# Gated linear attention: where a chunk's state work stands on VectorE, and ACT's copy of the turned keys

## The chip, the core and the metric

One core of one Trainium2 chip runs one program. The metric is the device time of the whole program in microseconds (us), the median of several executions. Names of engines: TensorE is PE, VectorE is DVE, ScalarE is ACT, GpSimd is POOL, SyncE is SP.

## The reference, cut to what matters

The program computes two layers of a trunk; layer 1 has, beside a recurrent branch (LRU), a gated linear attention (GLA) in both directions, over 1024 latent tokens and 128 context tokens. The change touches only the GLA chunks of that layer. What they compute, for one direction:

```python
def step(S, inp):
    qx, kx, vx, ax = inp
    b = jnp.cumsum(ax, axis=1)
    diff = b[:, :, None] - b[:, None, :]
    decay = jnp.where(causal, jnp.exp(jnp.minimum(diff, 0.0)), 0.0)
    scores = jnp.einsum('bthc,bshc,btshc->btsh', qx, kx, decay)
    o = jnp.einsum('btsh,bshe->bthe', scores, vx) + jnp.einsum('bthc,bhce->bthe', qx * jnp.exp(b), S)
    b_last = b[:, -1]
    S_new = jnp.exp(b_last)[..., None] * S + jnp.einsum('bshc,bshe->bhce', kx * jnp.exp(b_last[:, None] - b), vx)
    return S_new, o
```

Scores and output within a chunk need no state. The state S goes from chunk to chunk, once forward and once backward.

## The kernel before

The tokens stand in nine tiles of 128 (TILES = 9): eight of latents and, last, the context tile, for which the state is cleared. The program treats each as a chunk, v = 0 to 8, with all four heads and both directions at once. The forward direction takes tile v, the backward direction tile 7 - v (and 8 for v = 8).

The decay between two tokens depends on both, so the scores of a chunk are built by halving, in seven levels. At level `step` the tile is cut into blocks of 128, 64, ... 2 tokens, and each block's two halves are scored against each other with the decay taken from the block's middle. For each level:
- POOL forms the differences to the middle, in two operations (L2933, L2934);
- ACT takes their exponential (L2985; the widest level has its own, L2974 and L2975);
- DVE multiplies them with the queries and keys, in two operations, one for each half of the blocks (`factors`, L3007 and L3008, "factors of level n");
- PE multiplies the factors (`level`, L3112);
- DVE puts the products into the score tile `wsum` by mask (`put`, L3023; level 0, the diagonal, L3021).

Tiles and PSUM banks of the levels are double buffered by the level's parity: factors of level n wait for PE's level n - 2, level n waits for put n - 2. DVE's queue has, in every step, the factors of level step + 2 and then the put of level step.

The state's work of a chunk stands around it. ACT makes the state's exponentials (`state_exp`). POOL weighs queries and keys with them (`weigh`, L2914, once for each direction, behind its differences of levels 3 and 4), and copies the sums of the next chunk (`copies`, L2921 and L2922) behind level 6. PE turns the weighed keys (`turn_keys`, L3121) between levels 5 and 6, into PSUM bank 6, and ACT copies them out (`keep_kT`, L2962). Behind level 7 PE has a row of work that I call the tail: queries with the backward state (`from_state`, L3129, into its own bank), the two products of keys and values for the new states (`into_state`, L3139, backward into bank 6, forward into bank 7), level 0 of the next chunk (L3105), queries with the forward state (L3129), scores with values (`out`, L3149). Then comes level 1 of the next chunk. DVE adds the products to the states one chunk later (`new_state`, L3050, four operations for each direction), keeps the backward output (`backward_out`, L3035 or L3037) and, from chunk 4 on, the forward output (`add_o`, L3057; for chunks 0 to 3 ACT's `keep_o` does that). For chunks 0 to 3 a low part of the LRU's output is made on DVE too (L3074, from ACT's copy L2996).

Nothing is scheduled by a planner: every engine has its instructions in the order in which the functions below write them, and semaphores tie them. The waits that matter here:

```python
def turn_keys(v):
    for d in range(2):
        pe.wait_ge(gt_weighed[d], v + 1)
    pe.wait_ge(gt_S_new[1], v)
```

`from_state(v, 1)` waits for `gt_b_kept` (backward output of chunk v - 1) and `gt_S_new[1]`, `into_state` for `gt_kT_kept` and `gt_S_new`, `keep_kT` for `gt_turned` and `gt_u`.

Of the kernel before, what the change touches and what calls it, by code (L numbers as in the profile page):

```python
# [13 lines left out]
ALU = mybir.AluOpType  # L14
# [7 lines left out]
SAMPLE_TILES, TILES = 8, 9  # L22
# [51 lines left out]
def trunk(nc, A):  # L74
    st = ExitStack()
    with st:
# [54 lines left out]
        AT = Region(AT0, WT0)("AT", [P, 2, KD, T], F32R)  # L131
# [9 lines left out]
        ATf = AT[:].bitcast(F32)  # L141
# [1368 lines left out]
        def passing(v):  # L1510

            return (v, 7 - v) if v < CTX else (CTX, CTX)
# [1343 lines left out]
        lru_high = sem_of("lru_high")  # L2856
# [7 lines left out]
        def o_is_first(v):  # L2864

            return v < SAMPLE_TILES // 2
# [75 lines left out]
        def chunk_scalar(act):  # L2942
            def state_exp(v, d, part):
                tile = passing(v)[d]
                V = gate_sum[:, 2 * d:2 * d + 2, tile, 1 - d:GT - d]
                end = gate_end[:, 2 * d:2 * d + 2, tile]
                if part == 0:
                    act.wait_ge(gt_weighed[d], v)
                    if v > 1:
                        act.wait_ge(gt_S_new[d], v - 1)  # L2950
                    nc.scalar.activation(gt_E[d][:, 2 - 2 * d:4 - 2 * d, :], V, ACT.Exp, scale=1.0 / TAU)
                    nc.scalar.activation(gt_decay[v % 2][d][:, :], end, ACT.Exp)
                    return
                for ct in range(2):
                    ins = nc.scalar.activation(gt_E[d][:, 2 * d + ct, :], V[:, ct, :], ACT.Exp, scale=-1.0 / TAU, bias=end[:, ct:ct + 1])
                ins.then_inc(gt_exp[d], 1)

            def keep_kT(v):
                act.wait_ge(gt_turned, v + 1)
                for d in range(2):  # L2960
                    act.wait_ge(gt_u[d], v)
                    ins = nc.scalar.activation(gt_kT[d][:].rearrange("p c n -> p (c n)"), psum[:, T_BANK, 2 * d * P:2 * (d + 1) * P], ACT.Copy)  # L2962
                ins.then_inc(gt_kT_kept, 1)

            def keep_o(v):
                act.wait_ge(wi_o[v % 2], v // 2 + 1)
                nc.scalar.activation(h_sum[:, :, v * P:(v + 1) * P], psum[:, O_BANK, :].rearrange("p (h n) -> p h n", h=4), ACT.Copy, scale=GK ** -0.5).then_inc(o_kept, 1)

            def widest(v):

                act.wait_ge(wi_F[1], per_level(v, 1))
                for q in range(4):
                    V = gate_sum[:, q, v, 1 - q // 2:GT - q // 2]
                    nc.scalar.activation(gl_E[1][:, q, 0:P // 2], V[:, 0:P // 2], ACT.Exp, scale=-1.0 / TAU, bias=gate_mid[0][:, q, v:v + 1])  # L2974
                    ins = nc.scalar.activation(gl_E[1][:, q, P // 2:P], V[:, P // 2:P], ACT.Exp, scale=1.0 / TAU, bias=gate_mid[1][:, q, v:v + 1])  # L2975
                ins.then_inc(wi_E[1], 1)

            for v in range(TILES):
                for step in range(1, NL + 1):
                    p = step % 2  # L2980
                    if step == 1:
                        widest(v)
                    else:
                        act.wait_ge(wi_D[p], per_level(v, step) + 1 if p == 0 else 3 * v + (step - 1) // 2)
                        nc.scalar.activation(gl_E[p][:, :, :], gl_E[p][:, :, :], ACT.Exp, scale=1.0 / TAU).then_inc(wi_E[p], 1)  # L2985
                    if step == 1 and v and o_is_first(v - 1):
                        keep_o(v - 1)
                    if step == 1:
                        state_exp(v, 0, 0)
                    if step == 2:  # L2990
                        state_exp(v, 0, 1)
                        state_exp(v, 1, 0)
                    if step == 3:
                        state_exp(v, 1, 1)
                    if step == 4 and v < 4:
                        nc.scalar.activation(AT[:, 0, v, :], ATf[:, 1, v, :], ACT.Copy).then_inc(lru_high, 1)  # L2996
                    if step == 6:
                        keep_kT(v)

        def chunk_vector(dve):  # L3000
            def factors(v, step):
                s, B, p = v % 2, LEVELS[step - 1], step % 2
                H = B // 2
                F, E, G = halves(gl_F[p][:, :, :], B), halves(gl_E[p][:, :, :], B), halves(gl_kqk[s][:, :, :], B)
                dve.wait_ge(wi_E[p], per_level(v, step) + 1)
                dve.wait_ge(wi_mm[p], per_step(v, step))
                nc.vector.tensor_tensor(F[:, :, :, 0:H], E[:, :, :, 0:H], G[:, 0:4, :, 0:H], ALU.mult)  # L3007
                nc.vector.tensor_tensor(F[:, :, :, H:B], E[:, :, :, H:B], G[:, 2:6, :, H:B], ALU.mult).then_inc(wi_F[p], 1)  # L3008
# [16 lines left out]
            def first_factors(v):  # L3025
                dve.wait_ge(wi_in[v % 2], 64 * (v // 2) + 64)
                factors(v, 1)

            def backward_out(v):
                tile = passing(v)[1]  # L3030
                hs, part = h_sum[:, :, tile * P:(tile + 1) * P], psum[:, B_BANK, :].rearrange("p (h n) -> p h n", h=4)
                dve.wait_ge(gt_b, v + 1)
                if tile != CTX and o_is_first(tile):
                    dve.wait_ge(o_kept, tile + 1)
                    nc.vector.scalar_tensor_tensor(hs, part, GK ** -0.5, hs, ALU.mult, ALU.add).then_inc(gt_b_kept, 1)  # L3035
                else:
                    nc.vector.tensor_scalar(hs, part, GK ** -0.5, None, ALU.mult).then_inc(gt_b_kept, 1)  # L3037

            def new_state(v, d):
                dve.wait_ge(gt_u[d], v + 1)  # L3040
                dve.wait_ge(gt_exp[d], v + 1)
                if d:
                    dve.wait_ge(gt_b, v + 1)
                else:
                    dve.wait_ge(wi_o[v % 2], v // 2 + 1)
                for ct in range(2):
                    for par in range(2):
                        r, c = slice(64 * par, 64 * par + 64), slice(par * P, (par + 1) * P)
                        S = gl_S[r, 2 * d + ct, c]
                        ins = nc.vector.scalar_tensor_tensor(S, S, gt_decay[v % 2][d][r, ct:ct + 1], psum[r, U_BANK[d], (2 * ct + par) * P:(2 * ct + par + 1) * P], ALU.mult, ALU.add)  # L3050
                ins.then_inc(gt_S_new[d], 1)

            def add_o(v):
                hs = h_sum[:, :, v * P:(v + 1) * P]
                dve.wait_ge(wi_o[v % 2], v // 2 + 1)
                dve.wait_ge(gt_b_kept, v + 1 if v == CTX else 8 - v)
                nc.vector.scalar_tensor_tensor(hs, psum[:, O_BANK, :].rearrange("p (h n) -> p h n", h=4), GK ** -0.5, hs, ALU.mult, ALU.add).then_inc(o_kept, 1)  # L3057

            def behind(v, step):

                if step == 0:
                    new_state(v, 1)
                elif step == 1:
                    new_state(v, 0)
                    if v == SAMPLE_TILES - 1:
                        for d in range(2):
                            dve.wait_ge(gt_S_new[d], SAMPLE_TILES)
                        nc.vector.memset(gl_S[:, :, :], 0.0).then_inc(S_reset, 1)
                        dve.wait_ge(S_reset, 1)
                elif step == 2 and not o_is_first(v):  # L3070
                    add_o(v)
                elif step == 3 and v < 4:
                    dve.wait_ge(lru_high, v + 1)
                    nc.vector.tensor_tensor(AT[:, 1, v, :], ATf[:, 1, v, :], ATf[:, 0, v, :], ALU.subtract)  # L3074
            first_factors(0)
            dve.wait_ge(wi_mask_in, 16)
            dve.wait_ge(S_in, 32)
            for v in range(TILES):
                for step in range(NL + 1):
                    if step + 2 <= NL:  # L3080
                        factors(v, step + 2)
                    if step == 0 and v:
                        backward_out(v - 1)
                    put(v, step)
                    if v:
                        behind(v - 1, step)
                if v + 1 < TILES:
                    first_factors(v + 1)
            backward_out(TILES - 1)
            for step in range(4):  # L3090
                behind(TILES - 1, step)

        def chunk_tensor(pe):
# [334 lines left out]
```

## Time and profile before

| what | value |
|---|---|
| median of 3 runs | 3427.88 us (3426.07 to 3429.23) |
| the profiled execution's own time | 3433.07 us |
| its span, first to last instruction | 3431.4 us |
| PE, DVE, ACT, POOL busy | 92%, 53%, 33%, 32% |
| DVE, POOL, ACT busy from 2240 to 2490 us | 163.92, 122.06, 82.54 us of 250 |

The share of the whole span says little on this stage: the matmuls of the dense layers fill most of the span, and the GLA chunks, some 236 us, have all four engines hand work to one another. The rows below are therefore read from that stretch.

### The profile page before, as it was taken

Reading aid. Unit: us, or ns where it says so; the run is one execution under the profiler, and the core shown is the slowest. Engines: PE = TensorE matmul, PEld = TensorE weight load, DVE = VectorE, ACT = ScalarE, POOL = GpSimd, SP = SyncE. Lnnn points to the kernel's source line nnn. Section 1 sums busy time; section 2 is a strip of 40 time slices with the busy share of each in tenths; the row PEclk is TensorE's granted clock in tenths of the full one; section 3 lists DMA queues with packets and bytes.
Section 4 is the critical chain, followed back from the end, with each engine's and each line's share of the span. In section 5 each row is a group of like instructions: output and inputs, shape, how many; then the busy total and the mean of one; then the engine's idle time right before and its main releaser. Section 6 shows DMA issues by size and latency. Waiting matters only on the chain.

```text
span 3431.4 us, 44437 instructions
## 1 busy us (share of the span) xinstructions
PE 3149.4 (92%) x17132; PEld 2766.5 (81%) x17132; DVE 1819.3 (53%) x2569; ACT 1130.5 (33%) x1920; POOL 1083.0 (32%) x700
## 2 busy tenths in 40 slices
PE   6899858899889999999999899867789999999998
PEld 2788737799768999999998898556668999999997
DVE  2699669555477333333335655466676333333335
ACT  2333224555454121112113476533254121112112
POOL 1376336110024332232321221145444232323231
PEclk8999979999999999999999999956699999999999
DMA  5556535000031111011104332321131111111103
GB/s 186 175 204 209 177 104 162 33 26 1 10 108 62 50 50 49 24 49 49 49 24 117 120 126 70 129 78 42 35 108 68 43 50 49 33 40 49 49 24 123
DMA packets 182342, 270.68 MB, mean 79 GB/s; under 512 B 16392, under 2 KB 105520, under 8 KB 182192
## 3 DMA queue, kind: packets, MB, share of 16 engines
q1 hardware_dynamic: 182192, 268.65, 23.5%
q8 instruction: 97, 1.59, 0.2%
q14 instruction: 53, 0.43, 0.0%
HBM read 221.43 MB, written 47.19 MB: 78 GB/s over the span
## 4 chain that ended last, share of the span: by engine, by line
PE 74%; DVE 12%; issue 4%; POOL 4%; ACT 2%; DMA 1%; SPq 1%; POOLq 0%; DVEq 0%; ACTq 0%
PE psum L847 23%; PE psum L874 20%; PE psum L685 6%; PE psum L1884 4%; PE psum L688 3%; PE psum L1068 3%; PE psum L1872 2%; PE psum L1879 2%; DVE ada_acc L298 2%; PE psum L2183 2%; DVE mix_x L2380 1%; PE psum L456 1%; PE psum L3112 1%; DVE mix_v L2393 1%; PE psum L2545 1%
## 5 line engine op out<-in xcount | busy, mean ns | idle before, releaser
L847 PE MATMUL psum<-AT,WF 128*128 128x384 f32 x4608 | 805.3, 334 | 0.0
L847 PEld LDWEIGHTS psum<-AT,WF 128*128 128x128 f32 x4608 | 800.1, 188 | 2.5 <-POOL WF L2340 0.3
L874 PE MATMUL psum<-WF,H 128*128 128x512 f32 x3024 | 691.1, 389 | 0.0
L874 PEld LDWEIGHTS psum<-WF,H 128*128 128x128 f32 x3024 | 567.2, 188 | 116.9
L953 DVE TENSOR_TENSOR yacc<-yacc,psum 128x512 f32 x504 | 346.8, 688 | 331.9 <-PE psum L874 331.9
L933 DVE TENSOR_TENSOR relu_t<-relu_t 128x384 f32<-128x384 f32 x192 | 163.4, 851 | 607.7 <-ACT relu_t L893 607.7
L966 POOL TENSOR_TENSOR H<-relu_t,H 128x384 fp32r<-128x384 f32 x192 | 192.4, 1030 | 496.6 <-ACT H L897 496.6
L962 POOL TENSOR_TENSOR WF<-RAW,WF 128x2048 fp32r<-128x2048 f32 x30 | 138.9, 4631 | 504.5 <-ACT WF L888 504.5
L893 ACT ACTIVATE relu_t<-psum 128x384 f32<-128x384 f32 x192 | 94.5, 492 | 593.9 <-PE psum L847 587.8
L685 PE MATMUL psum<-WT,AT 128*128 128x512 f32 (+1 forms) x1296 | 284.2, 380 | 0.0
L685 PEld LDWEIGHTS psum<-WT,AT 128*128 128x128 f32 x1296 | 233.5, 192 | 43.6
L888 ACT ACTIVATE WF<-RAW 128x2048 fp32r<-128x2048 f32 x30 | 57.6, 1919 | 588.5 <-PE psum L874 588.5
L621 POOL TENSOR_TENSOR WT<-RAW,WT 128x1024 fp32r<-128x1024 f32 (+3 forms) x34 | 115.4, 3419 | 359.3 <-ACT WT L610 359.3
L2183 PE MATMUL psum<-WT,AT 128*128 128x512 f32 x864 | 205.9, 398 | 3.6 <-POOL WT L2324 3.6
L298 DVE SCALAR_TENSOR_TENSOR ada_acc<-ada_raw,silu_c,ada_acc 128x512 f32<-128x512 f32 x126 | 193.4, 1535 | 4.5
L2183 PEld LDWEIGHTS psum<-WT,AT 128*128 128x128 f32 x864 | 164.0, 192 | 38.5 <-POOL WT L2324 4.4
L688 PE MATMUL psum<-AT,WT 128*128 128x384 f32 (+1 forms) x936 | 170.4, 340 | 0.0
L688 PEld LDWEIGHTS psum<-AT,WT 128*128 128x128 f32 (+1 forms) x936 | 159.7, 183 | 7.6 <-issue 0.3
L3112 PE MATMUL psum<-gl_F 64*128 64x64 f32 x1008 | 111.2, 390 | 53.4 <-DVE wsum L3023 37.3
L319 POOL TENSOR_TENSOR ada_acc<-ada_acc,ada_scaled 128x512 f32<-128x512 f32 x90 | 136.6, 1518 | 73.3 <-DVE ada_acc L291 49.3
L1884 PEld LDWEIGHTS psum<-vK,probT 128*128 128x128 f32 x1280 | 147.8, 192 | 14.3 <-ACT probT L1949 13.0
L1884 PE MATMUL psum<-vK,probT 128*128 128x64 f32 x1280 | 153.8, 275 | 1.1 <-ACT probT L1949 1.1
(353 smaller groups left out, 4291.8 us busy)
## 6 DMA issues: line engine op xcount, KB each, us to landing
RAW<-ffn_w SPq DMA_DIRECT2D x64, 1024.0 KB, 5.9
ada_raw<-ada_w SPq DMA_DIRECT2D x18, 2048.0 KB, 8.0
RAW<-w_in_even SPq DMA_DIRECT2D x5, 2048.0 KB, 8.8
RAW<-w_in_odd SPq DMA_DIRECT2D x5, 2048.0 KB, 8.1
mix_x<-x_all SPq DMA_DIRECT2D x18, 512.0 KB, 3.3
feat_even<-stage SPq DMA_DIRECT2D x36, 256.0 KB, 4.2
x<-mix_x SPq DMA_DIRECT2D x18, 512.0 KB, 2.6
col_first<-ada_w SPq DMA_DIRECT2D x4, 2048.0 KB, 15.3
```

Of the source, the lines that this page charges most:

```text
L298: nc.vector.scalar_tensor_tensor(acc, w, c, acc, ALU.mult, ALU.add).then_inc(ada_part, 1)
L685: mm = nc.tensor.matmul(psum[:, s, 0:width], AT[:, a, k, rows_], wt(g, b, width)[:, k, :], start=first, stop=last)
L688: mm = nc.tensor.matmul(psum[0:feats, s, 0:TB], wt(g, a, width)[:, k, cols_], AT[:, b, k, s * TB:(s + 1) * TB], start=first, stop=last)
L847: mm = nc.tensor.matmul(psum[:, bank, 0:TB], w1_part[a][:, k, m * P:(m + 1) * P], AT[:, b, k, tb * TB:(tb + 1) * TB], start=(k == 0 and n ...
L874: mm = nc.tensor.matmul(psum[:, 3 + bank, :], H1[:, slot, a, m, ds(i * TB + (u // 2) * P, P)], w2_part[b][:, m, (u % 2) * 512:(u % 2 + 1) ...
L933: nc.vector.tensor_tensor(relu_t[:, tb, :], relu_t[:, tb, :], relu_t[:, tb, :], ALU.mult).then_inc(square_ready[tb], 1)
L953: nc.vector.tensor_tensor(y, y, psum[:, 3 + bank, :], ALU.add).then_inc(down_kept[bank], 1)
L962: nc.gpsimd.tensor_tensor(WF[:, 1, 1, :], w2_raw, WFf[:, 1, 0, :], ALU.subtract).then_inc(w2_low, 1)
L966: nc.gpsimd.tensor_tensor(H1[:, slot, 1, m, tb * TB:(tb + 1) * TB], relu_t[:, tb, :], H1f[:, slot, 0, m, tb * TB:(tb + 1) * TB], ALU.subtr ...
L1884: mm = nc.tensor.matmul(psum[:, 6, 0:HD], probT[:, n % 2, b * P:(b + 1) * P], vK[:, b, 64 * (n % 2):64 * (n % 2) + 64], start=(b == 0), st ...
L2183: mm = nc.tensor.matmul(psum[:, 2 * s + h, :], AT[:, a, k, t * P:(t + 1) * P], wt(8 * l + N_GROUPS + h, b, 512)[:, k, :], start=(k == 0 an ...
L3112: mm = nc.tensor.matmul(blocks(out)[:, :, cols], F, blocks(F)[:, :, cols], start=True, stop=True)
```

## The change

Three things move; nothing is added or taken away.

```diff
                     if step == 4 and v < 4:
                         nc.scalar.activation(AT[:, 0, v, :], ATf[:, 1, v, :], ACT.Copy).then_inc(lru_high, 1)
-                    if step == 6:
+                    if step == 7:
                         keep_kT(v)
...
             def behind(v, step):
 
-                if step == 0:
+                if step == 4:
                     new_state(v, 1)
-                elif step == 1:
+                elif step == 5:
                     new_state(v, 0)
                     if v == SAMPLE_TILES - 1:
                         for d in range(2):
                             dve.wait_ge(gt_S_new[d], SAMPLE_TILES)
                         nc.vector.memset(gl_S[:, :, :], 0.0).then_inc(S_reset, 1)
                         dve.wait_ge(S_reset, 1)
-                elif step == 2 and not o_is_first(v):
-                    add_o(v)
-                elif step == 3 and v < 4:
-                    dve.wait_ge(lru_high, v + 1)
-                    nc.vector.tensor_tensor(AT[:, 1, v, :], ATf[:, 1, v, :], ATf[:, 0, v, :], ALU.subtract)
+                    backward_out(v)
+                elif step == 6:
+                    if not o_is_first(v):
+                        add_o(v)
+                    if v < 4:
+                        dve.wait_ge(lru_high, v + 1)
+                        nc.vector.tensor_tensor(AT[:, 1, v, :], ATf[:, 1, v, :], ATf[:, 0, v, :], ALU.subtract)
...
                     if step + 2 <= NL:
                         factors(v, step + 2)
-                    if step == 0 and v:
-                        backward_out(v - 1)
+                    if step == 5 and v:
+                        behind(v - 1, 4)
                     put(v, step)
-                    if v:
+                    if step in (5, 6) and v:
                         behind(v - 1, step)
                 if v + 1 < TILES:
                     first_factors(v + 1)
-            backward_out(TILES - 1)
-            for step in range(4):
+            for step in range(4, 7):
                 behind(TILES - 1, step)
```

DVE in chunk 1, first half, before (L3007 and L3008 are the factors, of levels 2, 3 and 4; L3050 the state updates of chunk 0):

```order
L3037 TENSOR_SCALAR h_sum<-psum 128x4x128
L3021 SCALAR_TENSOR_TENSOR wsum_214<-psum,ident 128x512
L3050 SCALAR_TENSOR_TENSOR gl_S<-gl_S,gt_decay_225,psum 64x128 x4
L3007 TENSOR_TENSOR gl_F_212<-gl_E_210,gl_kqk_202 128x16x16
L3008 TENSOR_TENSOR gl_F_212<-gl_E_210,gl_kqk_202 128x16x16
L3023 COPY_PREDICATED wsum_214<-level_mask,psum 128x512
L3050 SCALAR_TENSOR_TENSOR gl_S<-gl_S,gt_decay_224,psum 64x128 x4
L3007 TENSOR_TENSOR gl_F_211<-gl_E_209,gl_kqk_202 128x32x8
L3008 TENSOR_TENSOR gl_F_211<-gl_E_209,gl_kqk_202 128x32x8
```

In the changed kernel L3037 and both L3050 rows are gone from here. DVE in the same chunk, second half, changed (L3007 and L3008 are the factors of level 7; the first L3050 is the backward state's, of gt_decay_225; L3023 are puts 5, 6 and 7; the LRU line is L3076 here):

```order
L3007 TENSOR_TENSOR gl_F_212<-gl_E_210,gl_kqk_202 128x256
L3008 TENSOR_TENSOR gl_F_212<-gl_E_210,gl_kqk_202 128x256
L3050 SCALAR_TENSOR_TENSOR gl_S<-gl_S,gt_decay_225,psum 64x128 [waits stage0_29,stage0_19,stage0_23]
L3050 SCALAR_TENSOR_TENSOR gl_S<-gl_S,gt_decay_225,psum 64x128 x3
L3023 COPY_PREDICATED wsum_214<-level_mask,psum 128x512 [waits stage0_13,stage0_12]
L3050 SCALAR_TENSOR_TENSOR gl_S<-gl_S,gt_decay_224,psum 64x128 [waits stage0_15,stage0_18,stage0_22]
L3050 SCALAR_TENSOR_TENSOR gl_S<-gl_S,gt_decay_224,psum 64x128 x3
L3037 TENSOR_SCALAR h_sum<-psum 128x4x128 [waits stage0_29]
L3023 COPY_PREDICATED wsum_214<-level_mask,psum 128x512 [waits stage0_14,stage0_11]
L3076 TENSOR_TENSOR AT<-AT 128x1152 [waits stage0_35]
L3023 COPY_PREDICATED wsum_214<-level_mask,psum 128x512 [waits stage0_13,stage0_12]
```

Where three puts stood in a row behind the factors of level 7, the updates, the backward output and the LRU line now stand ahead of, between and behind them. PE's order is the same in both kernels. Its rows around the turn in the changed kernel, where line numbers are two higher (L3123 is the turn, L3114 are levels 5, 6 and 7; stage0_25 is gt_S_new[1], which the backward state update raises):

```order
L3114 MATMUL psum<-gl_F_212 128x16x4 [waits stage0_10,stage0_14]
L3114 MATMUL psum<-gl_F_212 128x16x4 x7
L3123 MATMUL psum<-ident,gt_W_220 128x128 [waits stage0_25,stage0_21,stage0_20]
L3123 MATMUL psum<-ident,gt_W_220 128x128
L3123 MATMUL psum<-ident,gt_W_221 128x128 x2
L3114 MATMUL psum<-gl_F_211 128x32x2 [waits stage0_9,stage0_13]
L3114 MATMUL psum<-gl_F_211 128x32x2 x7
L3114 MATMUL psum<-gl_F_212 128x64 [waits stage0_10,stage0_14]
L3114 MATMUL psum<-gl_F_212 128x64 x7
L3131 MATMUL psum<-gl_S,gt_W_221 128x256 [waits stage0_25,stage0_30]
```

Nothing moved here; what moved is the instruction on DVE that raises stage0_25.

## Rows read from the trace of the kernel before

**Rows 1.** The page: the span.

```profile
span 3431.4 us, 44437 instructions
```

**Rows 2.** Windows: stretch, length, busy time by engine, granted clock, DMA share, GB/s.

```profile
2421.22:2426.92 5.70, 4.91 (x38) 4.28 (x36) 2.25 (x5) 3.73 (x14) 1.36 (x3) 0.50 0.01 3
...
2268.36:2275.90 7.54, 7.54 (x35) 5.98 (x33) 1.37 (x3) 0.00 (x0) 1.24 (x2) 0.71 0.14 37
...
2351.39:2358.37 6.98, 6.98 (x34) 5.60 (x32) 1.37 (x3) 0.00 (x0) 1.25 (x2) 0.76 0.14 38
...
2426.92:2433.69 6.77, 6.77 (x34) 5.45 (x32) 3.13 (x7) 2.59 (x8) 1.25 (x2) 0.79 0.16 39
...
sum 56.15, PE 56.15 PEld 44.99 DVE 17.99 ACT 10.39 POOL 9.96; mean PE 7.02 PEld 5.62 DVE 2.25 ACT 1.30 POOL 1.24
```

**Rows 3.** The chain of waits in chunk 6: start, length, what.

```profile
2422.37 0.66 ACT gt_kT L2962 x2
2423.03 0.53 ACT gl_E L2985
```

**Rows 4.** Timeline, chunk 6: start, length, engine, instruction, idle before and releaser.

```profile
2412.63 1.46 POOL L2914 TENSOR_TENSOR gt_W<-gt_E,gt_kq 128x512 f32<-128x512 f32 x1
2413.61 1.42 DVE L3050 SCALAR_TENSOR_TENSOR gl_S<-gl_S,gt_decay,psum 64x128 f32<-64x128 f32 x4
...
2416.16 0.84 POOL L2933 TENSOR_TENSOR gl_E<-gl_I,gl_V 128x256 f32<-128x256 f32 x1 [0.69 <-DVE gl_F L3008]
...
2418.83 0.61 POOL L2922 COPY gl_I<-gate_sum 128x512 f32<-128x512 f32 x1
...
2420.38 1.03 POOL L2934 TENSOR_TENSOR gl_E<-gl_V,gl_I 128x256 f32<-128x256 f32 x1
...
2421.22 1.11 PE L3121 MATMUL psum<-ident,gt_W 128*128 128x128 f32 x4
...
2422.26 1.97 PE L3112 MATMUL psum<-gl_F 64*128 64x64 f32 x16
...
2422.91 0.63 ACT L2985 ACTIVATE gl_E<-gl_E 128x512 f32<-128x512 f32 x1
2423.57 0.43 DVE L3007 TENSOR_TENSOR gl_F<-gl_E,gl_kqk 128x256 f32<-128x256 f32 x1 [2.22 <-ACT gl_E L2985]
2423.92 0.42 DVE L3008 TENSOR_TENSOR gl_F<-gl_E,gl_kqk 128x256 f32<-128x256 f32 x1
...
2425.02 1.97 PE L3112 MATMUL psum<-gl_F 64*128 64x64 f32 x16 [0.79 <-DVE wsum L3023]
...
2426.92 2.07 PE L3129 MATMUL psum<-gl_S,gt_W 128*128 128x256 f32 x4
```

**Rows 5.** Timeline, chunk 3: POOL from its second weighing on, and the turn.

```profile
2335.75 1.27 POOL L2914 TENSOR_TENSOR gt_W<-gt_E,gt_kq 128x512 f32<-128x512 f32 x1
2337.72 0.73 POOL L2933 TENSOR_TENSOR gl_E<-gl_I,gl_V 128x256 f32<-128x256 f32 x1 [0.69 <-DVE gl_F L3008]
...
2340.57 0.85 POOL L2933 TENSOR_TENSOR gl_E<-gl_I,gl_V 128x256 f32<-128x256 f32 x1 [1.45 <-DVE gl_F L3008]
...
2343.23 1.81 POOL L2922 COPY gl_I<-gate_sum 128x512 f32<-128x512 f32 x1
...
2345.28 1.11 PE L3121 MATMUL psum<-ident,gt_W 128*128 128x128 f32 x4
2345.99 1.02 POOL L2934 TENSOR_TENSOR gl_E<-gl_V,gl_I 128x256 f32<-128x256 f32 x1
```

**Rows 6.** Timeline, chunk 0: POOL's last difference, level 6, last exponential, level 7.

```profile
2262.43 0.83 POOL L2934 TENSOR_TENSOR gl_E<-gl_V,gl_I 128x256 f32<-128x256 f32 x1
...
2263.70 1.97 PE L3112 MATMUL psum<-gl_F 64*128 64x64 f32 x16
...
2264.35 0.63 ACT L2985 ACTIVATE gl_E<-gl_E 128x512 f32<-128x512 f32 x1
...
2266.46 1.97 PE L3112 MATMUL psum<-gl_F 64*128 64x64 f32 x16 [0.79 <-DVE wsum L3023]
```

## The prediction, before the changed kernel ran

> **What bounds the kernel now.** I read the page first: 3431.4 us of span [rows 1]. The change touches one stage, the GLA chunks, nine of them in line, from about 2248 to 2484 us. So I read the windows of that stage, then its chain of waits, then its timeline. All times below are on the scale of the trace of before.
>
> In the windows the reader is to see two things. From the turn of the keys to the last level of chunk 6, TensorE runs at a granted share of 0.50, the lower of its two levels (1.2 of 2.4 GHz). And from the first state matmul of a chunk to the first level of the next, TensorE is busy without a gap: 56.15 us busy in 56.15 us, eight times 7.02 on average [rows 2]. That tail is one queue on TensorE, so whatever delays its first matmul (L3129) delays the next chunk by as much. The question is only when it starts.
>
> In the chain of waits, what stands ahead of the tail is ACT's copy of the turned keys and then, behind it on ACT's queue, the last exponential (L2985) [rows 3]. The timeline of chunk 6 shows the same piece: POOL's differences for the last level end at 2420.38 + 1.03 = 2421.41, the last exponential starts only at 2422.91 because the key copy stood ahead, VectorE's factors of level 7 end at 2424.34, level 7 on TensorE starts at 2425.02 and the tail at 2426.92 [rows 4].
>
> **What the change does to that piece.** It moves work, it adds none. The two state updates (four L3050 each, 1.42 us a set [rows 4]), the backward output and, in four chunks each, the forward output or the key of the LRU half leave the first half of a chunk and stand behind the factors of level 7. What decides is a wait that the diff does not touch. TensorE turns the keys between levels 5 and 6, into the PSUM bank that also holds the backward state's product, and so waits for the backward state update of the chunk before (gt_S_new[1]). Both updates were done by 2413.61 + 1.42 = 2415.03 [rows 4], 6 us before the turn; the backward one now stands behind the factors of level 7. On TensorE's queue the turn has levels 6, 7 and the whole tail behind it. So the new chain is: POOL's last difference, last exponential, factors of level 7, state update, turn, level 6, level 7, tail. The ACT move belongs to it: a key copy ahead of the last exponential would now wait for a turn that waits for that exponential.
>
> **Does the first half give the time back?** Only if POOL's last difference comes earlier. Chunks 5 to 8, with chunk 6 as the pattern [rows 4]: POOL's second weighing ends at 2412.63 + 1.46 = 2414.09. It hangs on the output matmuls of the chunk before and on POOL's own queue, not on the moved work, so it stays. From there to 2421.41 POOL is idle once, 0.69 us, waiting for factors that will now be ready. Taken away, that gives 0.69. But VectorE's factors and POOL's operations, both with two inputs in SBUF, now run side by side all the way, and they hold each other up: POOL's last difference took 1.03 us beside factors and 0.83 us where it was alone in chunk 0 [rows 4, 6], so about 0.19 for each half of a set of factors. Levels 4 and 5 bring four new such halves, 0.76 us. POOL ends at 2421.41 - 0.69 + 0.76 = 2421.5: nothing gained. Then, step by step: exponential 0.07 + 0.63 to 2422.2; factors 0.03 + 0.77 (2423.57 to 2424.34) to 2423.0; state update 1.42 to 2424.4; turn 1.04 (2421.22 to 2422.26) to 2425.4; level 6 and level 7, each 1.90 (2425.02 to 2426.92), to 2429.2. The tail starts at 2429.2, not 2426.92: **+2.2 us** a chunk, 8.9 for four.
>
> Chunks 1 to 4, with chunk 3 as the pattern [rows 5]: weighing ends at 2337.02, the last difference at 2347.01. In between lie idle times of 0.69 and 1.45, and a copy (L2922) of 1.81 us that takes 0.61 in chunk 6 [rows 4]; the 1.20 over it is the LRU key on VectorE, which also has two inputs in SBUF and now comes later. These 3.34 us go. Six more halves of factors beside POOL cost 1.14 (two of them ahead of the weighing). POOL ends at 2344.8, 2.2 earlier. Exponential 0.70, factors 0.80, update 1.42, turn 1.04, two levels 3.80 lead to 2352.55; the tail started at 2351.39 [rows 2]: **+1.15 us**, 4.6 for four.
>
> Chunk 0 has no update behind it. There the exponential no longer stands behind the key copy: it started at 2264.35, POOL was done at 2263.26. Level 7 then goes right behind level 6, at 2263.70 + 1.90 = 2265.6 and not 2266.46 [rows 6]: **-0.8 us**.
>
> **The clock in the tail.** The tail's length is set by where the clock rises: the product of length and granted share is 5.35 us in both end rows (7.54 x 0.71, 6.77 x 0.79) [rows 2]. TensorE now stands idle for some 5 us ahead of each turn and chunks take other lengths, so the rise falls elsewhere. I take a share of 0.72, 7.4 us against 7.02, as the rise has more room to be late than early: **+3.0 us** for eight. Bounds: all tails as the shortest, -2.0; all at 0.50 throughout, 10.7 us each, +29.
>
> Costed at nothing: the backward output, the second update, the outputs moved to step 6 and, in chunk 8, the clearing of the state. TensorE's turn and two levels (4.84 us) cover them. Put 5, the second update and the backward output stand in a row there; none is longer than a set of updates, so they come to at most 4.3. With the clearing, once, at most 5.7, so it costs 0 to 0.9; I take 0. Uncovered, each would cost its own length in every chunk. In the end the last backward output stands behind both updates, nothing to 0.7 us (half a set of updates), beside a DMA that ends later. SP's loads hang on the weighing, on the state products and on the outputs; their order stands, and they keep whole chunks in hand.
>
> Sum: 8.9 + 4.6 - 0.8 + 3.0 = 15.7 us. The profiled execution took 3433.07 us in all (1.7 around its span), so 3448.8; the median of the runs is 5.2 below it, hence 3443.6.
>
> [...] The row shows that VectorE and POOL each wait for the other's body alone: 0.2 us lost for a factor half whose record lasts 0.42 [rows 4]. [...]
>
> **Rivals.** (a) *Full blocking*: each added half costs 0.42, not 0.19. With 4 halves in four chunks and 6 in four that is 40 x 0.23 = +9.2: 3453. The mutual wait is in the rows, its size against it. Chance 0.08. (b) *No added contention*: the halves slip between POOL's operations. Then 0.76 a chunk and 1.14 a chunk come back, -7.6: 3436, at the edge of what can be told. Against it: where both have work, the rows show them alternate. Chance 0.08. (c) *Faster, through the clock*: what leaves the first half packs levels 2 to 5 so that the clock is still at its upper level at the turn. Turn and two levels then take half, -2.4 a chunk, -19; with the tail also at full clock (5.35, not 7.4) -16 more: 3408. It decides once the granted share between turn and tail is above about 0.85, where it eats the 15.7. Against it: the share there is 0.50 now with TensorE 86% busy (4.91 of 5.70) [rows 2], and in the changed kernel a pause of some 5 us precedes it. Chance 0.03. (d) *Clock low throughout the tail*: +29 in place of +3, 3470; chance 0.03, as all eight tails now see it rise. The forecast has 0.78; its own range is 3438 to 3450.
>
> **Numbers.** A measurement tells about 0.2%, 6.9 us, from no change. Slower: the forecast but a sliver, (a), (d), and half of (b): 0.91. Same: half of (b) and that sliver, 0.06. Faster: (c), 0.03. The range runs from (b) to (a): 3436 to 3453.
>
> **What would show it.** In the changed profile: the turn's matmuls (L3123 there) idle some 5 us before, released by VectorE's state update; the key copy behind the last exponential; POOL nearly without a pause from second weighing to last difference; that difference ending as late after the outputs as now in chunks 5 to 8, 2 us earlier in 1 to 4; chunks 5 to 7 longer by 2 to 3 us. I am wrong if the turn still starts within a microsecond of level 5's end, if POOL ends over 2 us earlier in chunks 5 to 8, or if the clock between turn and tail is not 0.50.

## The result and the profile after

| | before, same session | changed |
|---|---|---|
| median of 8 runs each | 3428.73 us (3426.07 to 3432.99) | 3437.94 us (3436.12 to 3440.73) |
| the profiled execution | 3433.07 us | 3436.84 us |

The ratio is 1.0028, 95% interval 1.0017 to 1.0039: slower by 9.2 us, or 0.28%.

The two profiled executions are only 3.8 us apart, because each reached the GLA stage at a time of its own: its first level starts at 2248.05 us before and at 2240.53 after, though the code ahead of it is the same. So the stage is compared by itself: ACT's first table load behind it (L2265) ends it in both. The span of the changed kernel:

```profile
span 3435.1 us, 44437 instructions
```

The row of the table load, changed kernel (the second start counts):

```profile
L2265 ACT ACT_TABLE_LOAD  x2: 1283/1283/1283, 947.3 to 2492.7; - x2
```

The same row of before:

```profile
L2265 ACT ACT_TABLE_LOAD  x2: 1283/1283/1283, 952.7 to 2487.7; - x2
```

From first level to table load the stage took 2487.7 - 2248.05 = 239.6 us before and 2492.7 - 2240.53 = 252.2 after: 12.6 longer. I cut each chunk in two, as the prediction did: ahead of the tail, and the tail. First the windows ahead of the tail, from a chunk's first level to L3131, changed kernel, chunks 3, 6 and 8, and the sum over all nine (columns as in [rows 2]):

```profile
2324.82:2346.16 21.34, 13.51 (x117) 12.21 (x116) 16.23 (x29) 9.73 (x26) 12.33 (x15) 0.58 0.16 44
...
2409.23:2428.52 19.29, 11.80 (x117) 10.69 (x116) 14.46 (x26) 6.02 (x18) 12.32 (x15) 0.61 0.17 48
...
2463.82:2481.66 17.84, 11.78 (x118) 10.66 (x117) 14.96 (x27) 3.18 (x6) 9.48 (x10) 0.62 0.00 1
...
sum 180.65, PE 115.33 PEld 104.27 DVE 135.97 ACT 68.93 POOL 111.56; mean PE 12.81 PEld 11.59 DVE 15.11 ACT 7.66 POOL 12.40
```

The same windows of before, which ended at L3129:

```profile
2330.99:2351.39 20.40, 13.92 (x117) 12.39 (x117) 16.56 (x29) 9.81 (x26) 12.77 (x15) 0.58 0.16 46
...
2409.74:2426.92 17.18, 12.76 (x117) 11.50 (x116) 13.52 (x26) 5.62 (x17) 11.90 (x15) 0.59 0.19 54
...
2457.62:2475.55 17.93, 11.91 (x118) 10.69 (x117) 14.07 (x27) 3.06 (x6) 8.96 (x10) 0.68 0.00 1
...
sum 171.38, PE 119.63 PEld 107.17 DVE 133.29 ACT 67.49 POOL 111.58; mean PE 13.29 PEld 11.91 DVE 14.81 ACT 7.50 POOL 12.40
```

POOL's busy time is the same to 0.02 us and TensorE's is even 4.3 lower, yet the stretches are 9.3 us longer together: TensorE waits more. (POOL's equal sum hides differences: 0.4 us less in each of chunks 1 to 4, 0.4 more in each of chunks 5 to 7 and 0.5 more in chunk 8.) Chunks 1 to 4 each took 0.94 more, 5 to 7 each 2.1 more, chunk 8 took 0.1 less, and chunk 0 took 0.7 less (19.60 against 20.31).

The tails of the changed kernel in chunks 3 and 6, then the stretch from turn to tail in chunk 6, and last the sum of the eight tails, to hold against 56.15 in [rows 2]:

```profile
2346.16:2352.69 6.53, 6.53 (x34) 5.27 (x32) 1.65 (x4) 0.00 (x0) 1.25 (x2) 0.82 0.14 40
2428.52:2436.52 8.00, 8.00 (x34) 6.12 (x33) 2.73 (x6) 2.17 (x7) 1.25 (x2) 0.67 0.12 33
2423.89:2428.52 4.63, 4.62 (x36) 4.19 (x36) 3.88 (x8) 3.50 (x14) 0.00 (x0) 0.50 0.02 4
sum 60.48, PE 60.48 PEld 47.15 DVE 17.52 ACT 8.70 POOL 9.97; mean PE 7.56 PEld 5.89 DVE 2.19 ACT 1.09 POOL 1.25
```

The tails are busy without a gap, as before, and hold the same work; only the granted share differs: 6.53 x 0.82 and 8.00 x 0.67 are both 5.36. At the end the changed kernel is shorter: from the last chunk's L3131 to the table load 11.1 us against 12.1.

The timeline of chunk 6, changed kernel, answers to [rows 4]:

```profile
2412.31 1.26 POOL L2914 TENSOR_TENSOR gt_W<-gt_E,gt_kq 128x512 f32<-128x512 f32 x1
...
2418.28 0.83 DVE L3008 TENSOR_TENSOR gl_F<-gl_E,gl_kqk 128x256 f32<-128x256 f32 x1
2418.80 1.02 POOL L2933 TENSOR_TENSOR gl_E<-gl_I,gl_V 128x256 f32<-128x256 f32 x1
...
2419.78 0.84 POOL L2934 TENSOR_TENSOR gl_E<-gl_V,gl_I 128x256 f32<-128x256 f32 x1
...
2420.65 0.63 ACT L2985 ACTIVATE gl_E<-gl_E 128x512 f32<-128x512 f32 x1 [2.86 <-POOL gl_E L2934]
...
2421.31 0.76 DVE L3007 TENSOR_TENSOR gl_F<-gl_E,gl_kqk 128x256 f32<-128x256 f32 x1 [1.54 <-ACT gl_E L2985]
2421.99 0.41 DVE L3008 TENSOR_TENSOR gl_F<-gl_E,gl_kqk 128x256 f32<-128x256 f32 x1
2422.33 1.42 DVE L3050 SCALAR_TENSOR_TENSOR gl_S<-gl_S,gt_decay,psum 64x128 f32<-64x128 f32 x4
...
2423.89 1.09 PE L3123 MATMUL psum<-ident,gt_W 128*128 128x128 f32 x4 [3.82 <-DVE gl_S L3050]
...
2424.91 3.68 PE L3114 MATMUL psum<-gl_F 64*128 64x64 f32 x32
2425.02 0.66 ACT L2962 ACTIVATE gt_kT<-psum 128x256 f32<-128x256 f32 x2 [3.74 <-PE psum L3123]
```

Read it downward from POOL's last difference (2419.78 + 0.84 = 2420.62): exponential, factors, state update (to 2423.75) and turn each start within 0.15 us of the end of the one above; and the turn had been waiting 3.82 us for just that update. Levels 6 and 7 then go through as one row of 32. In this execution the chunk began 0.50 us earlier than in before; on the scale of before POOL ends at 2421.12 (predicted 2421.5), the factors at 2422.9 (2423.0), the turn starts at 2424.4 (2424.4) and the tail at 2429.0 (2429.2).

The wait of the turn (L3123) for the state update over the whole program, in us and times, changed kernel:

```profile
  DVE gl_S L3050: 29.1, 8
```

### The profile page after: what moved, and what is told of

Its sections match the earlier page's. It is cut to its first block, busy times and chain, and to the rows that moved or that the text cites. A ratio compares the mean times of both kernels' runs of the same rounds, so it can differ in the third digit from the quotient of the medians.

```text
span 3435.1 us, 44437 instructions
## 1 busy us (share of the span) xinstructions
PE 3140.5 (91%) x17132; PEld 2758.9 (80%) x17132; DVE 1820.5 (53%) x2569; ACT 1130.6 (33%) x1920; POOL 1085.4 (32%) x700
## 4 chain that ended last, share of the span: by engine, by line
PE 74%; DVE 11%; POOL 6%; issue 4%; ACT 2%; DMA 1%; SPq 1%; POOLq 1%; DVEq 0%; ACTq 0%
PE psum L847 23%; PE psum L874 20%; PE psum L685 6%; PE psum L1884 4%; PE psum L688 3%; PE psum L1068 3%; PE psum L1872 2%; PE psum L1879 2%; DVE ada_acc L298 2%; PE psum L2183 2%; DVE mix_x L2380 1%; PE psum L456 1%; DVE mix_v L2393 1%; PE psum L2545 1%; PE psum L3114 1%
## 5 line engine op out<-in xcount | busy, mean ns | idle before, releaser
L3114 PE MATMUL psum<-gl_F 64*128 64x64 f32 x1008 | 106.9, 383 | 37.9 <-DVE wsum L3023 24.4
```

Of the source, the lines that this page charges most:

```text
L3114: mm = nc.tensor.matmul(blocks(out)[:, :, cols], F, blocks(F)[:, :, cols], start=True, stop=True)
```

## The experiments

Each difference is against the kernel named. "Ahead" is the sum over nine chunks from first level to tail (171.4 before, 180.7 changed), "tails" the sum of eight (56.1 and 60.5).

**The state update one step earlier** (changed kernel; VectorE now has it behind the factors of level 6 and ahead of put 4).

```diff
-                    if step == 5 and v:
+                    if step == 4 and v:
                         behind(v - 1, 4)
```

> The changed kernel with one edit: the backward state update stands behind the factors of level 6, ahead of put 4, instead of behind the factors of level 7; all else as changed. Theory W (the turn of the keys waits for that update, and the update waits for the last exponential): the update then hangs on the exponential of level 6, which comes some 4 us before the last one, the turn hardly waits any more, and the first half keeps what the change freed. About 20 us under the changed kernel, 3414 to 3422, under the kernel before too. Rival C (the loss is what VectorE's factors and POOL's operations cost each other in the first half, and the turn's wait only takes up slack): that contention is the same here, so the time stays within 3 us of the changed kernel, 3435 to 3441.

Measured 3416.67 us against 3428.82 for before, ratio 0.9971 [0.9960, 0.9981]; ahead 156.8, tails 59.8. Its timeline in chunk 6, and its wait at L3123 over all chunks:

```profile
2404.36 1.97 PE L3114 MATMUL psum<-gl_F 64*128 64x64 f32 x16 [0.72 <-DVE wsum L3023]
2405.29 1.42 DVE L3050 SCALAR_TENSOR_TENSOR gl_S<-gl_S,gt_decay,psum 64x128 f32<-64x128 f32 x4
2406.86 1.09 PE L3123 MATMUL psum<-ident,gt_W 128*128 128x128 f32 x4 [0.52 <-DVE gl_S L3050]
2407.87 3.68 PE L3114 MATMUL psum<-gl_F 64*128 64x64 f32 x32
```

```profile
  DVE gl_S L3050: 4.6, 8
```

The wait fell from 29.1 to 4.6 us, and the sum ahead by 23.9. So the loss was the place of the update, and not the move out of the first half: with the wait gone the three moves together gain 12 us on before (the key copy alone gives 4 of them, next experiment). The rival, contention, fell.

**The key copy alone** (before, with ACT's copy at step 7).

```diff
-                    if step == 6:
+                    if step == 7:
                         keep_kT(v)
```

> The kernel before with only ACT's copy of the turned keys moved behind the last exponential; VectorE as before. Theory W: the copy held the exponential back by up to 1.1 us in chunks 0 and 5 to 8, and where it did, PE's level 7 now starts up to 0.8 us earlier: 1 to 4 us under the kernel before, 3425 to 3428. Rival A (the ACT move itself is a part of the loss, because the copies now come later and the state products wait for them): slower than before, by about the 0.5 us of an exponential in each of 9 chunks, 3433.

3424.86 us, ratio 0.9988 [0.9979, 0.9997]; ahead 166.4: chunk 0 by 0.7 less, chunks 5 to 8 by 1.06 each, chunks 1 to 4 nothing. Tails 59.0 in the profiled execution: 2.9 of the 5.0 went to the clock. In chunk 6 TensorE now has no gap from level 5 to the tail, and its clock stays at the lower level all the same (columns as in [rows 2]):

```profile
2413.86:2420.42 6.56, 6.56 (x53) 6.00 (x53) 4.50 (x7) 3.93 (x14) 3.27 (x5) 0.50 0.01 2
```

**The turn into the other bank** (changed kernel; the turn goes to bank 5 and waits for the backward output, which goes back to step 0, and no longer for the state; queries with the backward state, which write the same bank, wait in turn for ACT's copy of the turned keys).

```diff
-        T_BANK = 6
+        T_BANK = 5
...
-                pe.wait_ge(gt_S_new[1], v)
+                pe.wait_ge(gt_b_kept, v)
```

> The changed kernel with the wait taken from the turn: the keys are turned into the bank of the backward output, which is free once that output is kept, and the backward output stands in step 0 again, as before the change. The updates stay behind the factors of level 7. Theory W: without the wait the late update costs next to nothing; the turn starts at the end of level 5, levels 6 and 7 follow as in the kernel before: 3418 to 3428. Rival C: the order of factors against POOL is the same, 3435 to 3441.

3425.14 us, ratio 0.9989 [0.9980, 0.9998]; ahead 165.1, tails 60.8. The turn starts 10.8 us after the first level in chunks 5 to 7, not 14.7. Chunk 6:

```profile
2418.46 1.42 DVE L3050 SCALAR_TENSOR_TENSOR gl_S<-gl_S,gt_decay,psum 64x128 f32<-64x128 f32 x4
2419.91 0.72 DVE L3023 COPY_PREDICATED wsum<-level_mask,psum 128x512 f32<-128x512 int32 x1
...
2420.69 1.98 PE L3117 MATMUL psum<-gl_F 64*128 64x64 f32 x16 [1.53 <-DVE wsum L3023]
```

The wait moved: with the update still behind the factors of level 7, put 5 comes after it, and level 7 waits 1.53 us for put 5. This gains 15.6 us ahead of the tails, and the update at step 4, which has no such wait, 23.9; the backward output in step 0, which also differs, was not tried by itself.

**The backward update alone** (before, the key copy at step 7, and only `new_state(v - 1, 1)` behind the factors of level 7).

```diff
-                if step == 0:
+                if step == 4:
                     new_state(v, 1)
...
+                    if step == 5 and v:
+                        behind(v - 1, 4)
                     put(v, step)
```

> The kernel before with the backward update alone moved behind the factors of level 7 (and ACT's copy behind the last exponential, without which the two would wait for each other). Forward update, backward output, forward output and the LRU line stand as before; the clearing for the last chunk stands behind the moved update. Theory W: all of the loss is in this move, and the other moved work no longer gives anything back, so it is slower than the changed kernel: 3440 to 3450. Rival C: one update less in the first half, little added contention, within 4 us of the kernel before.

3450.02 us, ratio 1.0063 [1.0049, 1.0077]; ahead 187.0, tails 63.4. Against the key copy alone that one step costs 20.6 us ahead of the tails. The other moves gave 6.4 back: 1.4 in each of chunks 1 to 4, where the LRU key leaves the first half, and 0.1 to 0.3 in the others.

**The next chunk's copies behind POOL's last difference** (changed kernel).

```diff
-                    if step == 6 and v + 1 < TILES:
+                    if step == 7 and v + 1 < TILES:
                         copies(v + 1)
```

> The changed kernel with one edit on POOL: the copies of the next chunk's sums stand behind the differences of the last level instead of ahead of them. Theory P (in the changed kernel the turn hangs, over update, factors and exponential, on POOL's queue, which runs without a pause): the 1.7 us of three copies leave the chain in 8 chunks, up to 13 us less, 3424 to 3430. Rival D (VectorE's own row of work behind the factors is what ends last, POOL has slack): within 2 us of the changed kernel, 3436 to 3440.

3433.51 us against 3430.20, ratio 1.0013 [1.0004, 1.0022]. Some 4 to 6 us under the changed kernel, where 8 to 14 were expected; the intervals of the two ratios overlap, and the gain is clear only in the trace: ahead 176.1 for 180.7, 0.6 less in each of chunks 1 to 7. Its timeline in chunk 6:

```profile
2416.30 0.84 POOL L2933 TENSOR_TENSOR gl_E<-gl_I,gl_V 128x256 f32<-128x256 f32 x1 [0.36 <-DVE gl_F L3008]
...
2418.96 0.61 POOL L2922 COPY gl_I<-gate_sum 128x512 f32<-128x512 f32 x1
2419.01 0.84 DVE L3007 TENSOR_TENSOR gl_F<-gl_E,gl_kqk 128x256 f32<-128x256 f32 x1
2419.77 0.84 DVE L3008 TENSOR_TENSOR gl_F<-gl_E,gl_kqk 128x256 f32<-128x256 f32 x1
```

Without the copies POOL waits 0.36 us for factors; and POOL, now free to go on, works beside the factors of level 7, which take 1.60 us (2419.01 to 2420.61) and not 1.09 (2421.31 to 2422.40). Both stand on the chain, and they eat 0.87 of the 1.7 us that the copies took.

**Both: other bank and late copies.** The edits of the two kernels above together.

> The kernel with the keys turned into the other bank (no wait of the turn for the update) and POOL's copies behind the last differences. Theory P: there level 7 hangs on the last exponential and that on POOL, so it is 5 to 10 us under the 3425.1 of the kernel with the other bank alone, 3415 to 3420. Rival D: within 2 us of it.

3418.78 us against 3430.20, ratio 0.9971 [0.9960, 0.9983]; ahead 160.3, tails 59.4. The two gains ahead of the tails add up: 15.6 and 4.6 singly, 20.3 together.

**TensorE kept busy in the wait** (changed kernel, backward output at step 0). The three kernels with such an edit add matmuls whose result is overwritten at once, and leave nothing out.

```diff
+                pe.wait_ge(gt_b_kept, v)
+                for n in range(12):
+                    nc.tensor.matmul(psum[:, B_BANK, 0:P], ident[:, :], ident[:, :], start=True, stop=True)
                 pe.wait_ge(gt_S_new[1], v)
```

> The changed kernel with 12 matmuls of the identity with itself between level 5 and the turn, into the bank of the backward output (which stands in step 0 again, so that the bank is free; the result is overwritten). They add work to TensorE in a stretch in which it stands idle for some 5 us. Theory K (turn, levels 6 and 7 and most of the tail run at half the clock only because TensorE stood idle before): the granted share between turn and tail rises from 0.50 to near 1.00, each of the 4.8 us there takes half and the tail is shorter, 15 to 28 us less in all, 3410 to 3423. Rival N (the clock does not follow such a filling, or the added matmuls delay the turn by what they give): 3435 to 3445.

3415.00 us against 3430.20, ratio 0.9964 [0.9950, 0.9978]. Timeline and windows of chunk 6 (turn to tail, tail):

```profile
2405.79 5.46 PE L3125 MATMUL psum<-ident 128*128 128x128 f32 x24
2411.07 0.62 PE L3129 MATMUL psum<-ident,gt_W 128*128 128x128 f32 x4
2411.62 2.00 PE L3117 MATMUL psum<-gl_F 64*128 64x64 f32 x32
```

```profile
2411.07:2413.55 2.48, 2.48 (x37) 2.25 (x36) 1.29 (x4) 1.82 (x8) 0.00 (x0) 0.99 0.00 0
2413.55:2418.94 5.39, 5.39 (x35) 4.45 (x33) 3.57 (x8) 3.86 (x14) 1.25 (x2) 1.00 0.18 49
```

From the turn on TensorE has its upper level: turn and two levels take 2.48 us, not 4.63, and each tail 5.39. The matmuls outlast the wait they fill: the turn starts 16.1 us after the first level in chunks 5 to 7, not 14.7, and the kernel gains all the same.

**The same with the update at step 4**, and eight such matmuls.

```diff
-                    if step == 5 and v:
+                    if step == 4 and v:
                         behind(v - 1, 4)
...
+                for n in range(8):
+                    nc.tensor.matmul(psum[:, B_BANK, 0:P], ident[:, :], ident[:, :], start=True, stop=True)
```

> The kernel with the backward update ahead of put 4 (the first experiment) with 8 such matmuls between level 5 and the turn, the backward output in step 0. There TensorE waits only about a microsecond at the turn, so they cost some 2 to 3 us a chunk before they give anything. Theory K: the clock rises in most chunks, and it comes out 0 to 9 us under the first experiment's 3416.7, 3408 to 3417. Rival N: 8 times 2 us over it, 3430.

3404.47 us against 3430.20, ratio 0.9926 [0.9912, 0.9939]: the fastest kernel of the study, faster than both before and changed, and 4 us under the expected range. Ahead 162.3; added matmuls and turn in chunk 6, and the eight tails:

```profile
2399.46 3.23 PE L3125 MATMUL psum<-ident 128*128 128x128 f32 x16
2402.53 0.60 PE L3129 MATMUL psum<-ident,gt_W 128*128 128x128 f32 x4
```

```profile
sum 43.07, PE 43.07 PEld 35.58 DVE 23.83 ACT 18.19 POOL 9.97; mean PE 5.38 PEld 4.45 DVE 2.98 ACT 2.27 POOL 1.25
```

Against the update at step 4 without them, the matmuls cost 5.5 us ahead of the tails, give 16.7 in the tails and 1.9 at the end. There was hardly a wait to fill: without them the turn waited 0.52 us, and with them it starts 2.5 to 3.0 us later in chunks 5 to 7.

**The same matmuls in before**, eight ahead of its turn.

```diff
+                pe.wait_ge(gt_b_kept, v)
+                for n in range(8):
+                    nc.tensor.matmul(psum[:, B_BANK, 0:P], ident[:, :], ident[:, :], start=True, stop=True)
```

> The kernel before, with the 8 matmuls of the identity between level 5 and the turn, nothing moved. There TensorE does not wait at the turn, so they stand on its path: about 3.2 us a chunk at half the clock, and the copy of the keys, ahead of the last exponential on ACT, comes that much later too. Theory M (filling gives only where TensorE would stand idle, or where the moved update has made room): slower than, or at best like, the kernel before, 3428 to 3455. Rival F (the filling alone is what the fast version lives on, and the moved work has no part in it): near its 3404.5, below 3412.

3449.87 us (3437.72 to 3453.75) against 3430.65, ratio 1.0057 [1.0040, 1.0074]. In chunk 6:

```profile
2396.12 1.97 PE L3112 MATMUL psum<-gl_F 64*128 64x64 f32 x16 [0.42 <-DVE wsum L3023]
2398.02 3.27 PE L3120 MATMUL psum<-ident 128*128 128x128 f32 x16
2401.13 0.60 PE L3124 MATMUL psum<-ident,gt_W 128*128 128x128 f32 x4
...
2404.43 1.11 PE L3112 MATMUL psum<-gl_F 64*128 64x64 f32 x16 [1.66 <-DVE wsum L3023]
```

The matmuls push the turn back, by 2.9 to 3.6 us in chunks 5 to 7, and with it ACT's key copy and the last exponential behind that copy; so level 7 waits 1.66 us, not the 0.79 of [rows 4]. In the profiled execution, at 3437.7 us the fastest by 11, the stretches ahead of the tails grew by 17.8 us to 189.2 and the tails gave back 7.7. Stretch and tail together, chunks 1, 2, 3, 5 and 6, whose tails ran at a share of 1.00, came out even, 0.8 us less in all; chunks 0, 4 and 7, with tails at 0.70 to 0.79, and chunk 8 lost 10.8.

The missing wait does not set this kernel far apart from the one before it, whose turn had waited 0.52 us and was pushed back almost as far. What hangs on the turn differs: in before the last exponential does, over ACT's key copy, and in the changed order it does not. The same matmuls in the kernel with the key copy alone would have tried that by itself; they were not run.

**Both kernels looked at again.**

> The kernel before, unchanged, for a second profile. Theory T (the tails of eight chunks differ from execution to execution with where the clock rises, and the first profile, 56.1 us in sum, was a short one): stretches from a chunk's first level to its tail as before, 171.4 us in sum within 0.3, and tails of 57 to 61. Rival S (the sum of tails belongs to the kernel): 56 again.

> The changed kernel, unchanged, for a second profile. Theory T: 180.7 us in sum ahead of the tails, within 0.3, and tails of another sum than 60.5, between 57 and 64. Rival S: 60.5 again, within 0.5.

> The kernel before, unchanged, for a third profile. Theory T: tails between 56 and 62 in sum, and not the sum of the second profile. Rival S: 56 again.

They took 3428.35, 3436.75 and 3430.04 us. The tails of before in these two further executions, and those of the changed kernel in a second one:

```profile
sum 56.06, PE 56.06 PEld 44.99 DVE 17.97 ACT 10.33 POOL 9.95; mean PE 7.01 PEld 5.62 DVE 2.25 ACT 1.29 POOL 1.24
```

```profile
sum 56.11, PE 56.11 PEld 45.02 DVE 17.97 ACT 10.33 POOL 9.94; mean PE 7.01 PEld 5.63 DVE 2.25 ACT 1.29 POOL 1.24
```

```profile
sum 59.16, PE 59.16 PEld 46.78 DVE 17.50 ACT 8.68 POOL 9.96; mean PE 7.39 PEld 5.85 DVE 2.19 ACT 1.08 POOL 1.25
```

The sums ahead of the tails agree within 0.1 us for either kernel. The tails of before agree too: that they would differ by chance from one execution to the next was wrong for before. Those of the changed kernel were 60.48 and 59.16, so the clock's share of the loss is 3.0 to 4.4 us.

## Why the prediction was right, and where it was off

The forecast was 3443.6 us with a range of 3436 to 3453; the median is 3437.9. The sign and the mechanism held, the sum was too large: +15.7 where 9.2 were measured.

*The new chain* (last difference, exponential, factors of level 7, update, turn, two levels, tail) is what the timeline shows, and the update at step 4 and the other bank show it as the cause: both take that wait away, and both turn the loss into a gain. The wait is 3.8 us in chunks 1 to 7, where the forecast had some 5.

*Chunks 5 to 8, +2.2 each.* Right for 5 to 7: +2.1. Inside the term two sizes were off and nearly cancel. The added contention was costed at 0.76 us on POOL; POOL's busy time in chunk 6 grew by 0.42 (11.90 to 12.32), so POOL ended 0.4 earlier than the sum had it, 0.3 earlier than before. And the factors of level 7 took 1.09 us, not 0.77, because POOL's next differences stood beside them, which the forecast had not costed. The two levels took 3.61 us, not 3.80.

*Chunk 8 is the step that failed.* I let chunk 6 stand for it: +2.2 where it came out at -0.1, 2.3 of the 6.5 us that the sum was too high. Two things differ there. The first is in the trace of before:

```profile
2463.19 0.91 DVE L3068 MEMSET gl_S<- 128x1024 f32 x1 [0.28 <-DVE gl_S L3050]
...
2464.98 0.84 POOL L2933 TENSOR_TENSOR gl_E<-gl_I,gl_V 128x256 f32<-128x256 f32 x1 [1.63 <-DVE gl_F L3008]
```

In before the clearing of the state stood in the first half of chunk 8 and held POOL up by 1.63 us, not 0.69; I had costed the clearing only at its new place, and not credited its old one: chunk 8 took 17.93 there, 0.75 more than chunk 6. The second: it is the last chunk, so POOL makes no copies in it. In before that gave nothing, because the last exponential stood behind the key copy, 2.4 us after POOL's last difference; in the new chain POOL counts. The changed kernel:

```profile
2472.88 1.02 POOL L2934 TENSOR_TENSOR gl_E<-gl_V,gl_I 128x256 f32<-128x256 f32 x1
...
2477.03 1.09 PE L3123 MATMUL psum<-ident,gt_W 128*128 128x128 f32 x4 [2.37 <-DVE gl_S L3050]
```

The last difference ends 10.08 us after the first level, and not 11.39 as in chunk 6, and the turn waits 2.37 us, not 3.82. The two make 0.75 + 1.45 = 2.2.

*Chunks 1 to 4, +1.15 each.* Measured +0.94, 3.8 for 4.6. POOL ended 2.6 us earlier in chunk 3, where the forecast had 2.2.

*Chunk 0, -0.8.* Measured -0.7; the key copy alone shows the same -0.7, so it is the exponential no longer standing behind that copy.

*The clock in the tail, +3.0.* Measured +4.4 and +3.1 in two executions. The granted share between turn and tail is 0.50, as the forecast had it. But the reason that the prediction hints at, TensorE standing idle ahead of the turn, is not shown, and the key copy alone speaks against it: there the same instructions follow level 5 without a gap, busy 6.56 of 6.56 us, and the share is 0.50 too. What raised it was more work of another kind: behind 3.1 us of added matmuls the turn ran at 1.00 in the same chunk of before, again with no gap ahead. That activity raises the clock agrees with the Trainium skill (TensorE: Matmul & The Clock Gate, "Part 1: The HAM clock gate"), by which activity releases a throttle that is on by default. What it is about the added matmuls that does it, no run here separates.

*Not in the sum*: the end of the stage came out 1.0 us shorter, and the part of the program behind the table load another 1.3 (942.4 us in both executions of the changed kernel, 943.7 in all three of before). The cause is open: the key copy alone has 942.3, the changed kernel with late copies 943.7. The sum was 6.5 us too high. Chunk 8 explains 2.3 of it, chunks 1 to 4 0.8, chunks 5 to 7 0.3, these two ends 2.3; chunk 0 takes 0.1 back and the clock 0.1 to 1.4. That leaves some 1 to 2 us open. The stage begins at times 7 us apart in executions with like code ahead of it, so profiles can't settle so little.

*The rivals.* (a), full blocking, fell. Chunk 6 of the changed kernel has both cases in a row: POOL's difference beside a factor half took 1.02 us (2418.80), the next, alone, 0.84 (2419.78). That is 0.18 for a half, as [rows 4, 6] had it, and not 0.42. The Trainium skill (SBUF — State Buffer, "Who interferes with whom") names the contention of a two-input VectorE instruction with GpSimd, and the rows agree; that one blocks the other for a whole instruction it states of VectorE's two-port modes, and these factor halves did not cost POOL that. (b), no added contention, gave 3436, near the measured time, but for the wrong reason: had it held, chunks 5 to 7 would have been only 1.4 longer, and POOL's busy time the same. What POOL lost, 0.42 us in chunk 6, lies between (b) and the forecast's 0.76. (c) did not happen by itself, but the added matmuls show that its price is real: where the clock is up at the turn, turn and two levels take 2.48 us and the tail 5.39, and the kernel is 15 us faster than before. (d) did not happen.

## What to carry to other kernels

Before an instruction is moved later on its engine, look up who waits for the semaphore that it raises, and follow that queue to its end: here nothing but the place of a 1.42 us update decided between 9 us lost and 12 us gained. Let a chunk stand for others only after the first and the last have been held against it. And where TensorE runs a chain of short dependent steps at its lower clock, added matmuls ahead of it can be worth more than the time they push it back, as they were with a wait of 3.8 us and with one of 0.5. Before trying, look up what else hangs on the instruction that is pushed back: in before, where ACT's last exponential does, eight such matmuls cost 19 us.

## What the runs showed of the hardware that was not expected

- A busy TensorE did not have its upper level for that: in the changed kernel it was busy from turn to tail for 4.62 of 4.63 us at a share of 0.50, and in the key copy alone for 6.56 of 6.56 us, with no gap ahead. Behind the twelve added matmuls (5.46 us) the same instructions ran at 0.99.
- The tail's length times its granted share is 5.3 to 5.4 us in every kernel, from 5.39 x 1.00 to 8.00 x 0.67: TensorE is busy in it throughout, and the clock alone sets its length.
- POOL and VectorE hold each other up in both directions: with POOL's copies moved beside them, the factors of level 7 took 1.60 us instead of 1.09, and 0.77 where POOL stood still ([rows 4]). POOL's difference took 1.02 us beside a factor half and 0.84 alone.
